# Two-block transformer kernel: in the second block's attention the plain heads go first, and q and k blocks are turned inside it

## The chip, the cores and the metric

One Trainium2 chip, one core. The metric is the device time of one execution in microseconds. Engines by their names: PE is TensorE, ACT ScalarE, DVE VectorE, POOL GpSimd, SP SyncE. All data are fp32; the large projections split each operand into a high and a low fp32r part and make three matmuls of them, attention works in plain fp32.

## What is computed

The reference runs a first block (latent attention and sparse attention, gated, and an MLP) and then a second block of two layers, which is what the change touches:

```
for layer in range(2):
    h = rms_norm(x, g_mix[layer])
    qa, ka, va, qb, kb, vb, qc, kc, vc = split(h @ w_in[layer])    # 4 + 4 + 8 heads of 64
    o_a = differential(qa, ka, va)   # 4 heads: two softmaxes of 32 wide q and k; p0 - lam * p1, then @ v, then a norm per head
    o_b = moba(qb, kb, vb)           # 4 heads; at 512 tokens plain causal attention
    o_c = dilated(qc, kc, vc)        # 8 heads; one softmax with a mask of counts
    x = x + concat(o_a, o_b, o_c) @ w_out[layer]
    x = x + conv_gated_mlp(rms_norm(x, g_ffn[layer]))
```

512 tokens, model width 1024. q, k of each head get a partial rotation first. lam comes from four short vectors per layer by two dot products and two exponentials.

## The kernel before

One program per engine, written out by hand and tied together by counting semaphores. Tokens are four blocks of 128.

**Projection.** The last of six chunks of h @ w_in goes to PSUM banks 4 to 7, the one before it to banks 0 to 3. ACT copies each to z2 (`evacuate`, L1302) and signals `banks_drained`; DVE rotates q and k in z2 (L1727 to L1732) and signals `rotated` per chunk.

**Turning (`two_turns`, L625 to L631).** Attention needs q and k with the head dimension on partitions. Sixteen blocks of 128 columns are transposed by PE, four 128 x 128 transposes each (L889), over the 8 banks in turn, and taken from PSUM by ACT (L1311) or DVE (L1693). `apart` blocks are copied once per head mask: two copies with `halves`, four with `quarters` (the pairs' q); `whole` blocks, the k, once. Even blocks go to ACT, odd ones to DVE. Behind them `meet()` is a barrier of PE, ACT and DVE.

**Attention (`attend`, one version per engine; order by `Plan`, L500).** A job is a head. A score is one tile: 128 queries against the 1 to 4 key blocks of the causal triangle, in the order of query blocks 3, 0, 2, 1, so of 512, 128, 384 and 256 columns. One step issues one score:
- PE: score s (L926), into bank s mod 3; at step s + 3 the transposes of the probabilities (L941), two banks; two steps later their product with v (L952); then whatever `also(step)` holds. Each engine runs its own list in order, and PE does too.
- DVE: mask and row maximum (L1754), into a ring of `M_SLOTS` = 2; `join`; `also`; the copy of the transposed probabilities of query block 3 of single heads (L1774); every fourth value `finish` (L1797, L1803), which scales the head's output into O2.
- ACT: exponential and row sum (L1335), into a ring of `P_SLOTS` = 4 (8 for pairs); `also`; the other copies (L1349).

A head of the differential part is a pair: two scores per query block, lag 5 instead of 3, and `join` on DVE (L1789, L1790, L1792), per query block a reciprocal and a product of one column each, and then b * r + a over the tile. The first five steps behind the lag have filling matmuls, `FILL` = (6, 1, 1, 1, 1) (L899): ident against causal, into bank 7, a result that nobody reads.

`two_jobs` (L575): four pairs (steps 0 to 31), four plain heads (32 to 47), eight dilated heads (48 to 79). `o2_also` turns finished output blocks through bank 3 for the next projection: PE transposes at steps 51, 54, 57, 60, 64, 72, 80 (L1211, which waits until the block before has left the bank), ACT takes the high part one step later (L1576), DVE the low part two steps later (L2142). The norm of the pair heads is at steps 41 (ACT squares, L1581), 44 (DVE), 46 (ACT root, L1584), 48 (DVE). POOL splits weights (L391, L395) two slabs ahead and then waits for PE.

Of the kernel before, what the change touches and what calls it, by code (L numbers as in the profile page):

```python
# [26 lines left out]
D_MODEL, SEQ = 1024, 512  # L27
P = 128
# [65 lines left out]
def build(nc, xT_d, slabs_d, ada_d, c_d, cols_d, rows_d, consts_d, strips_d, pos_d, cpos_d,  # L94
# [5 lines left out]
    with ctx:  # L100
# [24 lines left out]
        rowsum = sb("rowsum", [P, 4, TT])  # L125
# [90 lines left out]
        ring_x = at("ring_x", 32768, [P, 4, SEQ])  # L216
        rope_2 = at("rope_2", 81920, [P, 4, 512])
# [74 lines left out]
        attended, combined = sem("attended"), sem("combined")  # L292
        turned = sem("turned")
# [202 lines left out]
        M_SLOTS, P_SLOTS, PT_SLOTS = 2, 4, 3  # L496
# [3 lines left out]
        class Plan:  # L500


            def __init__(self, jobs):
# [7 lines left out]
                n = len(self.scores)  # L511
                self.slots, self.before, last = [], [], {}
                for i, (m, c, j, v) in enumerate(self.scores):
# [5 lines left out]
                turn = 0  # L519
                for v, (m, j, i) in enumerate(self.values):  # L520
                    pair = len(jobs[m]["q"]) == 2
                    turn = max(turn, i + (PAIR_LAG if pair else TURN_LAG))
# [3 lines left out]
                    if pair:  # L526
                        self.joins.setdefault(i + COMBINE_LAG, []).append(v)
                self.steps = turn + 4

        def masked_slot(ring, u, n):  # L530
            return ring[0][:, u % M_SLOTS, 0:n]

        def probs_slot(ring, slot, n):
            return ring[0][:, M_SLOTS + slot, 0:n] if slot < P_SLOTS else ring[1][:, slot - P_SLOTS, 0:n]
# [41 lines left out]
        for h in range(4):  # L576
            two_jobs.append(job((T2a[:, 2 * h, :], T2a[:, 2 * h + 1, :]), T2b[:, 2 + h // 2, :],
                                lambda kb, h=h: z2[:, 1, kb, 64 * h:64 * h + 64],
                                O2[:, :, 768 + 64 * h:832 + 64 * h], causal))
        for h in range(4):  # L580
            two_jobs.append(job(T2[:, 12 + h, :], T2b[:, h // 2, :],
                                lambda kb, h=h: z2[:, 2, kb, 256 + 64 * h:320 + 64 * h],
                                O2[:, :, 512 + 64 * h:576 + 64 * h], causal))
# [5 lines left out]
        DIFF_SQ, DIFF_SUM, DIFF_ROOT, DIFF_SCALE = 41, 44, 46, 48  # L589
        O2_TURNS = [(51, 6, 4), (54, 7, 4), (57, 4, 6), (60, 5, 8), (64, 0, 10), (72, 1, 12), (80, 2, 14)]  # L590
# [40 lines left out]
        two_turn_chunk = [3] * 4 + [4] * 4 + [1] * 2 + [2] * 2 + [0] * 4  # L631
# [15 lines left out]
        def _(pe):  # L647
# [253 lines left out]
            def attend(jobs, ring, s_banks=S_BANKS, banks_ready=None, also=None):  # L901
# [13 lines left out]
                for step in range(plan.steps):  # L915
# [13 lines left out]
                    if TURN_LAG <= step < TURN_LAG + len(FILL):  # L929
                        release_clock(FILL[step - TURN_LAG])  # L930
# [260 lines left out]
            for layer in range(LAYERS):  # L1191
# [3 lines left out]
                def two_ready(n):  # L1195
                    pe.wait_ge(rotated, 5 * layer + two_turn_chunk[n] + 1)
                    if n in (0, 4):
# [1078 lines left out]
```

## Time and profile before

| | us |
|---|---|
| three runs, median (lowest to highest) | 2388.53 (2387.6 to 2389.87) |
| the profiled execution, its own time | 2389.8 |
| its span | 2388.0 |
| busy in the span: PE, PE weight load | 2285.1 (96%), 1819.2 (76%) |
| busy: DVE, ACT, POOL | 908.6 (38%), 619.4 (26%), 1385.3 (58%) |
| mean granted clock of PE | 0.988 of full |

Read the page from the top: busy time, then 40 slices of the span (the attention of the second block's two layers lies around 1108 to 1240 and 1811 to 1943 us), then the chain. In the timeline each line is a start, a length, the engine, the line of the kernel and what it writes and reads; like instructions are merged, with the first one's shape, and in brackets stands the idle time before, and who ended it. An fp32 matmul is two records.

### The profile page before, as it was taken

The page shows a single profiled execution, that of the slowest core. Times are in us where ns is not written, and L with a number is a line of the kernel's source. Part 1 is how long each engine was busy: PE and PEld are TensorE (multiplying, and loading weights), DVE is VectorE, ACT ScalarE, POOL GpSimd, SP SyncE. Part 2 cuts the span into 40 slices and gives each one's busy share as a digit, 9 for nine tenths or more (in the row PEclk, how much of TensorE's full clock was granted, in tenths as well). Part 3 has the DMA queues.
Part 4 walks back from the last instruction along what each step waited for, and adds up shares of the span by engine and source line. Part 5 has one row for each costly group of instructions (what it writes and reads, how often), then busy time and mean ns, then how long its engine had stood idle before and what let it go on. Part 6 is the DMA issues. An engine that isn't in the chain of part 4 may idle for free.

```text
span 2388.0 us, 29037 instructions
## 1 busy us (share of the span) xinstructions
PE 2285.1 (96%) x10645; PEld 1819.2 (76%) x10645; DVE 908.6 (38%) x1753; ACT 619.4 (26%) x1315; POOL 1385.3 (58%) x462
## 2 busy tenths in 40 slices
PE   4998899999999999999899999999999999999997
PEld 2787687777888888786687888887786787888885
DVE  6835786124111100433743433402425634333302
ACT  2243564012111100113651322301114632223200
POOL 3857501876677777675006777777673026777773
PEclk9999999999999999999999999999999999999998
DMA  8214211322122222122002222222221002222221
GB/s 337 85 71 159 104 57 54 108 100 92 71 99 95 88 102 96 71 96 81 1 2 71 89 105 88 88 106 88 72 104 53 1 19 71 97 97 88 96 98 53
DMA packets 32528, 206.02 MB, mean 86 GB/s; under 512 B 3888, under 2 KB 4144, under 8 KB 11440
## 3 DMA queue, kind: packets, MB, share of 16 engines
q1 hardware_dynamic: 32000, 200.27, 23.4%
q10 hardware_dynamic: 432, 4.46, 0.5%
q8 instruction: 62, 1.02, 0.2%
q14 instruction: 34, 0.28, 0.0%
HBM read 202.61 MB, written 2.10 MB: 86 GB/s over the span
## 4 chain that ended last, share of the span: by engine, by line
PE 83%; issue 7%; DVE 4%; POOL 3%; ACT 1%; DMA 1%; POOLq 0%; DVEq 0%; SPq 0%; ACTq 0%
PE PS L652 25%; PE PS L654 24%; PE PS L653 24%; PE PS L926 3%; PE PS L952 2%; PE PS L941 1%; DMA ada_first<-ada_dram 1%; POOL w_hi L391 1%; POOL w_lo L395 1%; DVE f_lo L1655 1%; PE PS L899 1%; PE PS L982 1%; PE PS L666 1%; DVE t L1624 1%; DVE ada_first L1816 0%
## 5 line engine op out<-in xcount | busy, mean ns | idle before, releaser
L391 POOL TENSOR_TENSOR w_hi<-raw,zero_c 128x2048 fp32r<-128x2048 f32 (+1 forms) x216 | 598.9, 2783 | 941.5 <-PE PS L654 907.3
L395 POOL TENSOR_TENSOR w_lo<-raw,w_hi 128x2048 fp32r<-128x2048 f32 (+1 forms) x216 | 757.4, 3517 | 12.6
L652 PE MATMUL PS<-f_hi,w_hi 128*128 128x512 f32 x1056 | 419.1, 397 | 5.5 <-DVE f_lo L1611 3.6
L654 PE MATMUL PS<-f_hi,w_lo 128*128 128x512 f32 x1056 | 417.8, 396 | 0.0
L653 PE MATMUL PS<-f_lo,w_hi 128*128 128x512 f32 x1056 | 414.7, 393 | 0.0
L652 PEld LDWEIGHTS PS<-f_hi,w_hi 128*128 128x128 f32 x1056 | 198.2, 188 | 52.8 <-issue 6.6
L654 PEld LDWEIGHTS PS<-f_hi,w_lo 128*128 128x128 f32 x1056 | 198.2, 188 | 49.9
L653 PEld LDWEIGHTS PS<-f_lo,w_hi 128*128 128x128 f32 x1056 | 198.2, 188 | 48.1
L2085 DVE SCALAR_TENSOR_TENSOR aux<-PS,cols,aux 128x510 f32<-128x510 f32 (+1 forms) x176 | 123.7, 744 | 237.1 <-ACT aux L1543 230.1
L652 PE MATMUL PS<-a_hi,w_hi 128*128 (+1 forms) x528 | 209.8, 397 | 0.0
L654 PE MATMUL PS<-a_hi,w_lo 128*128 (+1 forms) x528 | 208.9, 396 | 0.0
L653 PE MATMUL PS<-a_lo,w_hi 128*128 (+1 forms) x528 | 207.3, 393 | 0.0
L652 PE MATMUL PS<-w_hi,f_hi 128*128 128x512 f32 x384 | 154.8, 403 | 8.3 <-DVE t L1669 8.3
L653 PE MATMUL PS<-w_lo,f_hi 128*128 128x512 f32 x384 | 153.8, 401 | 0.0
L654 PE MATMUL PS<-w_hi,f_lo 128*128 128x512 f32 x384 | 153.7, 400 | 0.0
L1661 DVE TENSOR_TENSOR xT<-xT,PS 128x512 f32<-128x512 f32 x32 | 21.9, 685 | 284.8 <-PE PS L654 284.1
L654 PEld LDWEIGHTS PS<-a_hi,w_lo 128*128 128x128 f32 x528 | 99.1, 188 | 24.9
L653 PEld LDWEIGHTS PS<-a_lo,w_hi 128*128 128x128 f32 x528 | 99.1, 188 | 24.7 <-issue 0.2
L652 PEld LDWEIGHTS PS<-a_hi,w_hi 128*128 128x128 f32 x528 | 99.1, 188 | 23.0 <-issue 0.2
L952 PEld LDWEIGHTS PS<-z,ring 128*128 128x128 f32 x640 | 80.9, 192 | 18.5 <-ACT ring L1349 12.7
L652 PEld LDWEIGHTS PS<-w_hi,f_hi 128*128 128x128 f32 x384 | 73.4, 191 | 27.4 <-DVE t L1669 9.2
L1549 ACT ACTIVATE a_hi<-PS 128x512 f32 (+1 forms) x66 | 39.6, 599 | 208.4 <-DVE PS L2077 170.3
(387 smaller groups left out, 3610.6 us busy)
## 6 DMA issues: line engine op xcount, KB each, us to landing
raw<-slabs_dram SPq DMA_DIRECT2D x161, 1024.0 KB, 4.8
aux<-ada_dram SPq DMA_DIRECT2D x24, 512.0 KB, 3.8
ada_first<-ada_dram SPq DMA_DIRECT2D x4, 2048.0 KB, 21.7
cmpw<-cmpw_dram ACTq DMA_DIRECT2D x2, 2048.0 KB, 9.5
ada_late<-ada_dram SPq DMA_DIRECT2D x8, 512.0 KB, 3.6
xT<-xT_dram SPq DMA_DIRECT2D x1, 2048.0 KB, 15.9
out_dram<-t SPq DMA_DIRECT2D x4, 512.0 KB, 2.7
crow<-c_dram SPq DMA_DIRECT2D x1, 512.0 KB, 4.5
```

Of the source, the lines that this page charges most:

```text
L391: high = nc.gpsimd.tensor_tensor(w_hi[:, slot, c], raw[:, slot, c], zero[:, 0:c.stop - c.start], ALU.add)
L395: low = nc.gpsimd.tensor_tensor(w_lo[:, slot, c], raw[:, slot, c], w_hi[:, slot, c].bitcast(f32), ALU.subtract)
L652: nc.tensor.matmul(out, a_hi_, b_hi_, start=start, stop=False)
L653: nc.tensor.matmul(out, a_hi_, b_lo_, start=False, stop=False)
L654: return nc.tensor.matmul(out, a_lo_, b_hi_, start=False, stop=stop)
L666: last = nc.tensor.matmul(PS[:, 0, :], mean_w, t[:, k, :], start=not residual and k == 0, stop=k == ks[-1])
L899: nc.tensor.matmul(PS[:, 7, :], ident, causal, start=True, stop=True)
L926: nc.tensor.matmul(PS[:, step % s_banks, 0:128 * nb], jobs[m]["q"][c][:, 128 * j:128 * j + 128], jobs[m]["k"][:, 128 * lo:128 * (lo + nb)] ...
L941: last = nc.tensor.transpose(PS[:, S_BANKS + v % PT_BANKS, 128 * b:128 * b + 128], probs_slot(ring, plan.slots[i], 512)[:, 128 * b:128 * b ...
L952: last = nc.tensor.matmul(PS[:, 6 + m % O_BANKS, 64 * j:64 * j + 64], turned_slot(ring, v, 512)[:, 128 * b:128 * b + 128], jobs[m]["v"](lo ...
L1549: A(a_hi[:, fi, :], g.unsqueeze(1), ACT.Copy).then_inc(act_hi_ready, 1)
L2085: V.scalar_tensor_tensor(out=t[:, sh:], in0=PS[:, bank, 0:SEQ - sh], scalar=cols[:, ds(f + w, 1)], in1=t[:, sh:], op0=ALU.mult, op1=ALU.add)
```

## The change

- `two_jobs` starts with the four plain heads (steps 0 to 15); the pairs take steps 16 to 47, the dilated heads stay at 48 to 79.
- Of the sixteen blocks the four that the plain heads need (two of q in halves, two of k) are turned first, in banks 0 to 3. The other twelve are turned inside `attend` by `also`: PE at steps 0 to 7, 9, 11, 13 and 14, all in bank 3, each once the one before is taken; ACT or DVE takes it at the step after. The first score waits for the first four (`two_operands`), the score of step 16 for all sixteen.
- The barrier goes. DVE waits for ACT's small exponential on a new semaphore, `lam_ready`. The filling matmuls go from this attention (`fill=()`).
- Pairs: `join` works on two tiles at once, one reciprocal and one product over two columns of row sums, then the two wide operations. The lag is longer (joined two steps behind the second tile, transposed five and six behind it), the ring of probabilities has 10 slots, that of masked scores 3, in `ring_y`; `rowsum` has 8 rows.
- `Plan` holds each transpose at least three steps behind that of the fifth value before.
- The pair heads' norm moves to steps 58 to 64, the output turns to 56, 59, 63, 67, 70, 73, 80, in another order.

```diff
-        M_SLOTS, P_SLOTS, PT_SLOTS = 2, 4, 3
+        M_SLOTS, P_SLOTS, PT_SLOTS, P_PAIRS = 2, 4, 3, 10
...
                 for i, (m, c, j, v) in enumerate(self.scores):
-                    slot = i % (2 * P_SLOTS if len(jobs[m]["q"]) == 2 else P_SLOTS)
+                    pair = len(jobs[m]["q"]) == 2
+                    many = any(len(x["q"]) == 2 for x in jobs[max(0, m - 2):m + 1])
+                    slot = i % (P_PAIRS if many else P_SLOTS)
...
+                    slot = i % (M_SLOTS + 1 if pair else M_SLOTS)
+                    self.masks.append(slot)
+                    self.masked_before.append(last_mask.get(slot))
+                    last_mask[slot] = i
...
-                    pair = len(jobs[m]["q"]) == 2
-                    turn = max(turn, i + (PAIR_LAG if pair else TURN_LAG))
+                    if len(jobs[m]["q"]) == 2:
+                        i2 = i + (2 if v % 2 == 0 else 0)
+                        turn = max(turn, i2 + PAIR_LAG + v % 2)
+                        if v % 2:
+                            self.joins[i2 + COMBINE_LAG] = v
+                    else:
+                        turn = max(turn, i + TURN_LAG)
+                    if v >= PT_SLOTS + PT_BANKS:
+                        turn = max(turn, at_step[v - PT_SLOTS - PT_BANKS] + 3)
...
-        DIFF_SQ, DIFF_SUM, DIFF_ROOT, DIFF_SCALE = 41, 44, 46, 48
-        O2_TURNS = [(51, 6, 4), (54, 7, 4), (57, 4, 6), (60, 5, 8), (64, 0, 10), (72, 1, 12), (80, 2, 14)]
+        PAIRS_AT = 16
+        DIFF_SQ, DIFF_SUM, DIFF_ROOT, DIFF_SCALE = 58, 60, 62, 64
+        O2_TURNS = [(56, 4, 2), (59, 5, 4), (63, 0, 10), (67, 6, 8), (70, 7, 8), (73, 1, 12), (80, 2, 14)]
...
-        two_turns = [apart(i, two_src(3, 128 * i), T2, 2 * i, halves) for i in range(4)]
-        two_turns += [whole(i, two_src(4, 128 * i), P, T2[:, 8 + i, :], 1.0) for i in range(4)]
-        two_turns += [apart(i, two_src(1, 256 + 128 * i), T2, 12 + 2 * i, halves) for i in range(2)]
+        two_turns = [apart(i, two_src(1, 256 + 128 * i), T2, 12 + 2 * i, halves) for i in range(2)]
         two_turns += [whole(i, two_src(2, 128 * i), P, T2b[:, i, :], 1.0) for i in range(2)]
+        for i in range(4):
+            two_turns += [apart(i, two_src(3, 128 * i), T2, 2 * i, halves),
+                          whole(i + 1, two_src(4, 128 * i), P, T2[:, 8 + i, :], 1.0)]
         two_turns += [apart(i, two_src(0, 128 * i), T2a, 4 * i, quarters) for i in range(2)]
         two_turns += [whole(i, two_src(0, 256 + 128 * i), P, T2b[:, 2 + i, :], 1.0) for i in range(2)]
+        HEAD = 4
+        turn_step = {step: HEAD + n for n, step in enumerate((0, 1, 2, 3, 4, 5, 6, 7, 9, 11, 13, 14))}
...
-                turn(two_turns, ready=two_ready)
-                meet()
+                def two_turned(n):
+                    pe.wait_ge(turned_act, a0 + counts[n - 1][0])
+                    pe.wait_ge(turned_dve, d0 + counts[n - 1][1])
...
+                def two_operands(step):
+                    if step == 0:
+                        two_turned(HEAD)
+                    if step == TURN_LAG:
+                        pe.wait_ge(banks_drained, at_.drain)
+                    if step == PAIRS_AT:
+                        two_turned(len(two_turns))
...
                 def o2_also(step):
+                    if step in turn_step:
+                        two_turned(turn_step[step])
+                        two_transpose(turn_step[step], 3)
...
+                    if step - 1 in turn_step:
+                        two_taken(turn_step[step - 1])
...
-            def join(ring, plan, m, j, i, nb):
-
-                one, two = (rowsum[:, plan.sums[m][c] % 4, j:j + 1] for c in (0, 1))
-                r = ratio[:, i % 4:i % 4 + 1]
+            def join(ring, plan, jobs, v):
+
+                m = plan.values[v][0]
+                sel = slice(0, 4, 3) if v % 4 == 1 else slice(1, 3)
+                one, two = (rowsum[:, plan.sums[m][c] % 8, sel] for c in (0, 1))
+                r = ratio[:, v % 4 - 1:v % 4 + 1]
                 then(V.reciprocal(r, two))
                 then(V.scalar_tensor_tensor(out=r, in0=r, scalar=lam_c, in1=one, op0=ALU.mult, op1=ALU.mult))
-                a, b = (probs_slot(ring, plan.slots[i - 1 + c], 128 * nb) for c in (0, 1))
-                V.scalar_tensor_tensor(out=b, in0=b, scalar=r, in1=a, op0=ALU.mult, op1=ALU.add).then_inc(combined, 1)
+                for u in (v - 1, v):
+                    _, j, i = plan.values[u]
+                    _, nb = key_range(jobs[m], j)
+                    a, b = (probs_slot(ring, plan.slots[i - 1 + c], 128 * nb) for c in (0, 1))
+                    by = r[:, 1:2] if j > 1 else r[:, 0:1]
+                    V.scalar_tensor_tensor(out=b, in0=b, scalar=by, in1=a, op0=ALU.mult, op1=ALU.add
+                                           ).then_inc(combined, 1)
```

`two_taken(n)` exists on ACT and on DVE: it waits for `turned` and makes the copies of block n, from bank n for the first four and from bank 3 otherwise.

## Rows read from the trace of the kernel before

**Rows 1.** Busy time by stretch (us), the windows view: layer 0's stages, then layer 1.
```profile
1107.78:1120.20 12.42, 7.95 (x66) 7.02 (x65) 9.44 (x14) 11.64 (x20) 8.15 (x2) 0.98 0.32 128
1120.20:1162.62 42.42, 39.92 (x179) 25.44 (x180) 27.34 (x109) 22.84 (x72) 0.00 (x0) 0.97 0.02 8
1162.62:1187.51 24.89, 22.37 (x149) 17.64 (x148) 15.54 (x55) 15.12 (x48) 0.00 (x0) 1.00 0.00 1
1187.51:1239.52 52.01, 50.48 (x364) 42.18 (x364) 32.73 (x102) 33.97 (x104) 0.00 (x0) 1.00 0.01 1
...
1811.09:1942.59 131.50, 120.66 (x753) 92.11 (x751) 85.17 (x278) 83.57 (x243) 8.15 (x2) 0.99 0.04 14
```
In this view the columns are: stretch, length, busy time (and instructions) of PE, PE weight load, DVE, ACT, POOL, then granted clock, DMA share, GB/s.

**Rows 2.** Timeline, the turning ahead of layer 0's attention.
```profile
1108.01 1.91 PE L889 MATMUL PS<-consts,z 128*128 128x128 f32 x16
...
1109.08 2.73 DVE L1693 TENSOR_SCALAR T<-PS,small 128x512 f32<-128x512 f32 x4 [13.18 <-PE PS L889]
...
1112.16 2.41 ACT L1311 ACTIVATE T<-PS,small 128x512 f32<-128x512 f32 x4
```

**Rows 3.** Windows view again, the end of the turning and the first scores.
```profile
1117.50:1120.20 2.70, 0.02 (x1) 0.03 (x1) 2.51 (x4) 2.48 (x5) 0.00 (x0) 0.90 0.78 285
1120.20:1123.00 2.80, 2.80 (x4) 1.25 (x5) 0.92 (x3) 0.00 (x0) 0.00 (x0) 0.50 0.24 99
```

**Rows 4.** Windows view, eight steps of a pair head and four of single heads.
```profile
1143.90:1153.25 9.35, 8.45 (x47) 5.96 (x46) 7.53 (x31) 6.19 (x20) 0.00 (x0) 1.00 0.00 1
...
1219.04:1224.53 5.49, 5.49 (x40) 4.55 (x40) 3.31 (x12) 3.28 (x12) 0.00 (x0) 1.00 0.01 3
```

**Rows 5.** Instruction groups by line and shape, PE in 1120 to 1240: the filling matmuls.
```profile
L899 PE MATMUL PS<-consts 128*128 128x512 f32 x20 | 9.4, 592 | 0.0
```

**Rows 6.** Timeline, one turned output block and the step behind it.
```profile
1204.26 0.61 PE L1211 MATMUL PS<-consts,O 128*128 128x128 f32 x4
...
1204.70 0.81 PE L926 MATMUL PS<-T 128*128 128x384 f32 x2
...
1205.55 0.56 DVE L1754 CUSTOM_DVE_ANT_0 ring<-PS,strip 128x384 f32<-128x384 f32 x1 [0.94 <-PE PS L926]
...
1206.15 0.62 ACT L1335 ACTIVATE ring<-ring,negmax 128x384 f32<-128x384 f32 x1 [1.17 <-DVE negmax L1754]
...
1206.77 0.58 ACT L1576 ACTIVATE o_hi<-PS 128x512 fp32r<-128x512 f32 x1
```

**Rows 7.** Timeline, the scores of 512, 128 and 256 columns in steady state.
```profile
1219.04 1.08 PE L926 MATMUL PS<-T 128*128 128x512 f32 x2
...
1220.46 0.44 PE L926 MATMUL PS<-T 128*128 128x128 f32 x2
...
1222.99 0.65 PE L926 MATMUL PS<-T 128*128 128x256 f32 x2
```

**Rows 8.** Instruction groups by line and shape, masks and exponentials (busy us, mean ns, idle before).
```profile
L1754 DVE CUSTOM_DVE_ANT_0 ring<-PS,strip 128x512 f32<-128x512 f32 x8 | 5.5, 690 | 5.9 <-PE PS L926 5.9
...
L1754 DVE CUSTOM_DVE_ANT_0 ring<-PS,strip 128x256 f32<-128x256 f32 x8 | 3.4, 420 | 0.9 <-PE PS L926 0.9
...
L1754 DVE CUSTOM_DVE_ANT_0 ring<-PS,strip 128x128 f32<-128x128 f32 x8 | 2.3, 290 | 1.7 <-PE PS L926 1.2 <-issue 0.3
...
L1335 ACT ACTIVATE ring<-ring,negmax 128x512 f32<-128x512 f32 x20 | 14.4, 720 | 23.4 <-DVE negmax L1754 23.4
...
L1335 ACT ACTIVATE ring<-ring,negmax 128x128 f32<-128x128 f32 x20 | 7.9, 394 | 2.7 <-DVE negmax L1754 2.6
```

**Rows 9.** Windows view, a place in the first block's attention.
```profile
274.00:276.00 2.00, 1.29 (x12) 1.13 (x11) 1.81 (x6) 0.30 (x3) 2.00 (x2) 1.00 0.25 55
276.00:280.00 4.00, 4.00 (x17) 3.03 (x17) 3.14 (x11) 2.40 (x9) 3.46 (x7) 0.57 0.26 103
```

**Rows 10.** Timeline, a pair's join on DVE up to its wide operation.
```profile
1149.27 0.16 DVE L1789 RECIPROCAL stats<-rowsum 128x1 f32<-128x1 f32 x1
...
1149.80 0.75 DVE L1792 SCALAR_TENSOR_TENSOR ring<-ring,stats 128x512 f32<-128x512 f32 x1
```

More of the change, by code:

```diff
@@ L292, in build @@
         attended, combined = sem("attended"), sem("combined")
+        lam_ready = sem("lam_ready")
         turned = sem("turned")
@@ L576, in build @@
         for h in range(4):
+            two_jobs.append(job(T2[:, 12 + h, :], T2b[:, h // 2, :],
+                                lambda kb, h=h: z2[:, 2, kb, 256 + 64 * h:320 + 64 * h],
+                                O2[:, :, 512 + 64 * h:576 + 64 * h], causal))
+        for h in range(4):
             two_jobs.append(job((T2a[:, 2 * h, :], T2a[:, 2 * h + 1, :]), T2b[:, 2 + h // 2, :],
@@ L1568, in _, with two_taken @@
                 act.wait_ge(lam_summed, layer + 1)
-                A(small[:, 4:6], small[:, 4:6], ACT.Exp)
-                turn(two_turns)
-                meet()
+                A(small[:, 4:6], small[:, 4:6], ACT.Exp).then_inc(lam_ready, 1)
+                turn0 = at_.turn
+                def two_taken(n):
+                    _, _, acts, _ = two_turns[n]
+                    if acts:
+                        act.wait_ge(turned, turn0 + n + 1)
+                    for dst, scale in acts:
+                        A(dst, PS[:, n if n < HEAD else 3, :], ACT.Copy, scale=scale).then_inc(turned_act, 1)
+                for n in range(HEAD):
+                    two_taken(n)
+                at_.turn += len(two_turns)
                 m0 = at_.map
@@ L1751, in attend @@
                         dve.wait_ge(scores_ready, g0 + step + 1)
[L1752 to L1754 removed]
+                        if plan.masked_before[step] is not None:
+                            dve.wait_ge(probs_ready, g0 + plan.masked_before[step] + 1)
+                        V.tensor_tensor_reduce(out=masked_slot(ring, plan.masks[step], 128 * nb),
                                                in0=PS[:, step % s_banks, 0:128 * nb],
@@ L1758, in attend @@
                                                accum_out=negmax[:, step % 8:step % 8 + 1]).then_inc(scores_masked, 1)
-                    for v in plan.joins.get(step, ()):
-                        m, j, i = plan.values[v]
-                        _, nb = key_range(jobs[m], j)
-                        dve.wait_ge(probs_ready, g0 + i + 1)
-                        join(ring, plan, m, j, i, nb)
+                    if step in plan.joins:
+                        v = plan.joins[step]
+                        dve.wait_ge(probs_ready, g0 + plan.values[v][2] + 1)
+                        join(ring, plan, jobs, v)
                     if also:
@@ L2133, in _, with two_taken @@
                         dve.drain().then_inc(lam_summed, 1)
-                turn_counted(two_turns)
-                meet()
+                counts = turned_counts(two_turns)
+                turn0 = at_.turn
+                def two_taken(n):
+                    _, _, _, dves = two_turns[n]
+                    if dves:
+                        dve.wait_ge(turned, turn0 + n + 1)
+                    for dst, scale in dves:
+                        V.tensor_scalar(dst, PS[:, n if n < HEAD else 3, :], scale, None, ALU.mult
+                                        ).then_inc(turned_dve, 1)
+                for n in range(HEAD):
+                    two_taken(n)
+                at_.turn += len(two_turns)
+                at_.turn_a += counts[-1][0]
+                dve.wait_ge(lam_ready, layer + 1)
                 then(V.tensor_tensor(lam_c, small[:, 5:6], small[:, 4:5], ALU.subtract))
```

69 lines of the change are left out of this document (37 added, 32 removed).

## The prediction

> **What bounds the kernel now.** I read the page first: its table has PE busy nearly all the span, so a gain must come from a stretch where PE waits or does work that nobody needs. Next the busy time by stretch, cut at the marks of a layer's attention [rows 1]. The reader should see five stretches of layer 0, end to end: the turning of q and k up to the first score, 12.42 us, with PE busy 7.95; the four heads of pairs, 42.42 (32 score steps); the four plain heads, 24.89 (16 steps); the eight dilated heads, 52.01 (32 steps and the tail). Together 131.74 us; layer 1 takes 131.50, the last row. Everything that the change touches lies in these 2 x 131.7 us, 11% of the span. GpSimd's weight splits are far ahead there and cover nothing.
>
> Then the timeline, for what ends each wait. In the turning, PE makes 16 transposes in 1.91 us, and waits; ScalarE has to copy the last chunk first, load a table, do one small exponential, and takes its first blocks from 1112.16 on at 0.60 us each [rows 2]. In the last 2.70 us ahead of the first score PE does nothing, the granted clock falls, and the first 2.80 us of scores run at 0.50, the lower of the two levels (1.2 GHz) [rows 3]. In the steady stretches, four plain steps take 5.49 us with PE busy all the time, and eight steps of a pair head 9.35 us with PE busy 8.45 and VectorE 7.53 [rows 4]. So plain heads are bound by PE, pairs nearly so.
>
> **Part 1: the shorter opening.** PE transposes 4 blocks instead of 16 ahead of the first score (done at about 1109.9). The first score then waits for ScalarE's three copies: 1112.16 + 3 x 0.60 = 1113.97, with the hand-over 1114.1. VectorE's three, from 1109.1 on, end earlier. Opening: 1114.1 - 1107.8 = 6.3 us for 12.4. The barrier as such cost next to nothing: what ended it were the evictions of all 16. The new wait of VectorE for the exponential (lam_ready, 1112.3) lies ahead of the first mask and is covered by this wait for ScalarE.
>
> **Part 2: the filling matmuls go.** Ten fp32 matmuls of 512 columns, 20 records, 9.4 us [rows 5]. They lay in the first pair head, whose eight steps took 14.8 us (1120.2 to 1135.0) against 9.35 later. This gain is inside the 42.4 and is counted in parts 3 and 4, where I price the steps without them.
>
> **Part 3: twelve blocks turned inside the first sixteen steps.** This is the term that decides. All twelve use PSUM bank 3. At the end of step s PE waits until the block before has been taken from that bank, then transposes the next. That block is taken in step s only after the mask (VectorE) or after mask and exponential (ScalarE) of step s, and these need the score of step s, which PE can issue only behind the transposes of step s-1. So each step with a turn closes a loop over three engines. The trace has this loop once per output block, where it is three or more steps from the next and costs nothing [rows 6]: transposes at 1204.26, score at 1204.70 (+0.44), mask at 1205.55 (+0.85), exponential at 1206.15 (+0.60), copy at 1206.77 to 1207.35 (+0.62, +0.58): 3.09 us. The change puts such turns at steps 0, 1, 2, 3, 4, 5, 6, 7, 9, 11, 13, 14. Each interval is 0.44, the next step's score (1.08, 0.44, 0.86, 0.65 us for 512, 128, 384, 256 columns), its mask (0.69, 0.29, 0.56, 0.42), for ScalarE its exponential (0.72, 0.39, 0.62 for 512, 128, 384), the copies (0.60 on ScalarE or 0.69 on VectorE each; two for a block of halves, four for quarters, one for k) and 0.1 for the return to PE [rows 2, 6 to 8]:
> turn at 0, ScalarE 2 copies, step 1 of 128 columns: 2.86. At 1, VectorE 1, 384: 2.65. At 2, VectorE 2, 256: 2.99. At 3, ScalarE 1, 512: 3.63. At 4, 5, 6 again 2.86, 2.65, 2.99. From 7 to 9: 3.63. From 9, ScalarE 4, 384: 4.97. From 11, VectorE 4, 512: 5.07. From 13, ScalarE 1, 384: 3.17. From 14 to the first score of the pairs, VectorE 1, 256: 2.30. The sum is 39.8, with 0.9 for the first score 40.7 us.
> PE's own work in these steps is 4 x 5.49 + 12 x 0.44 = 27.2 us, so PE waits some 13 us, a little in every step. Where PE waited as much in the first block's attention, busy 1.29 us of 2, the granted clock then read a mean of 0.57 over 4 us, though PE was full again in them [rows 9]. I add 3.5 us: about 1.5 for the first stretch at the low clock behind the opening's 4.2 us of idle PE (before, idle for 2.70 brought a low stretch of 2.80 [rows 3]), and 2 for two or three later falls at 0.5 to 1 us of PE's share of a loop. Bounds: 0 (the clock holds) and 14 (it stays low for all 12 turns and 16 scores: 12 x 0.44 + 4 x 2.16 us more). Part 3: 44.2 us, where the four plain heads had 24.9.
> The Trainium skill (TensorE: Matmul & The Clock Gate, A second HAM failure mode: psum-queue depth-cycling) says that a PE which pauses often for a moment between groups of matmuls because it cycles through PSUM banks can see its clock swing between the levels, and it speaks against this change. The rows just named agree. By the rule taken fully the low clock holds through part 3; that is a rival below.
>
> **Part 4: pairs joined two tiles at a time.** A join spends 0.53 us in two tiny VectorE operations (1149.27 to 1149.80) ahead of the wide one [rows 10]; per head four such become two, so VectorE's 7.53 falls by 1.06 to 6.5, and a join is ready three steps ahead of its transposes instead of behind the next mask. Deeper rings (10 and 3 slots) take the other waits. PE becomes the bound. Its work without waits is the plain head's 5.49 plus a second set of scores, 2 x 1.08 = 2.16: 7.65. I take 8.0 per head and 1 for the change of lag: 33 us for four heads. Ends: 30.6 (7.65 each) and 37.4 (9.35 each, nothing gained).
>
> **Part 5: what is late next.** In the kernel before, the plain heads came behind the pairs and took 24.89 instead of 4 x 5.49 = 21.96: 2.9 us for the shorter lag, with a copy and its transposes late. Now the dilated heads stand there and pay it, and four values are turned in one step (53). The norm of the pair heads with its table loads moves from steps 41 to 48 to 58 to 64, and the output turns crowd from 51-80 to 56-80; both were inside the 52.0, at equal count. Dilated heads: 52.0 + 2.9 = 55 us, ends 53 and 57. The planner's new floor for a turn (three steps behind the fifth value before) binds nothing where all heads are plain, so the first block's attention keeps its order. No DMA and nothing on GpSimd moves; the weight split behind the attention starts later or earlier by as much as the attention ends.
>
> **Sum.** After: 6.3 + 44.2 + 33 + 55 = 138.5; before 131.7. Each layer is longer by 6.8, both by 13.6 us. The profiled execution took 2389.8 us (span 2388.0), so 2403.4; the median of the runs shown is 1.3 lower, and I forecast 2402.
>
> **The rivals.**
> Turns hidden (faster): PE never waits at bank 3, so part 3 costs PE's own 27.2 + 0.9 = 28.1. For it: an output turn with its wait costs nothing beyond PE's work in the trace. Against: those are at least three steps apart, and the loop of 2.7 to 3.6 us is twice PE's 1.37 + 0.44 per step. It decides if the loop is under 1.8 us. 6.3 + 28.1 + 33 + 55 = 122.4, minus 9.3 a layer: 2370. Chance 0.12.
> Balanced: the loop is as priced, but all else sits at its good end: no low clock, 6.3 + 40.7 + 31 + 53 = 131, minus 0.7 a layer: 2387. For it: in the plain stretch before, PE busy nine tenths kept the clock. Chance 0.20.
> Low clock through part 3: all 14 us instead of 3.5, 10.5 a layer more: 2402 + 21 = 2423. For it: the fall named above [rows 9]; against: there it came back within 4 us, while PE was full. By the Trainium skill (same page, What's actually happening) the slow clock is the default and activity lifts it, which is why half-filled steps could leave it low. Chance 0.10.
> The rings and the double join do not shorten the pairs (something else set 9.35, as ScalarE's chain): 4.4 a layer more, 2411. Chance 0.10.
> The forecast's own case, 2394 to 2409: 0.48.
>
> **How the numbers follow.** A difference under 0.2% (4.8 us) is about what a measurement of this kernel can't tell from none. Slower: 0.48 + 0.20 of the two slow rivals, and a little of the balanced case, 0.70. Same: most of the balanced case, 0.14. Faster: the hidden case and the rest of the balanced one, 0.16. The range 2382 to 2420 leaves out the hidden case and the worst of the low clock.
>
> **What would show it.** Right, if the first score comes 6 to 7 us behind the last projection matmul; if turns' transposes in the first eight steps are 2.6 to 3.7 us apart and the two blocks of quarters 5 us; if PE idles some 13 us per layer between score 0 and score 16, released by copies; if a pair head takes about 8 us. Wrong, if those transposes follow at 1.8 us, if score 16 comes within 30 us of score 0, or if the pairs still take 9.3.

## The result, and the profile after it

The changed kernel takes 2422.8 us (median of four runs, 2421.5 to 2426.0) against 2388.1 for the kernel before on the same chip (2386.5 to 2389.9): a ratio of 1.0148, 95% interval 1.0137 to 1.0160, slower by 34.7 us. The forecast was 2402 with a range up to 2420. The direction was right; the size was outside the range, 34.7 us where 13.6 stood in the sum. The execution shown here took 2421.5 us with a span of 2419.7; the one of before had 2388.0.

The windows view of the changed kernel, columns as in [rows 1]: opening, plain heads with the twelve turns, pairs, dilated heads of layer 0, then layer 1 whole.
```profile
1105.52:1111.46 5.94, 1.91 (x18) 1.67 (x16) 3.67 (x4) 5.55 (x9) 5.62 (x2) 0.89 0.29 121
1111.46:1158.36 46.90, 33.09 (x170) 25.16 (x171) 20.57 (x53) 18.64 (x52) 2.49 (x1) 0.76 0.06 23
1158.36:1197.89 39.53, 36.11 (x185) 26.15 (x185) 26.19 (x100) 23.25 (x75) 0.00 (x0) 0.91 0.00 1
1197.89:1254.10 56.21, 51.78 (x364) 42.20 (x364) 35.06 (x110) 35.85 (x107) 0.00 (x0) 1.00 0.01 1
1827.95:1974.40 146.45, 121.84 (x733) 93.66 (x731) 85.56 (x262) 83.17 (x243) 8.11 (x2) 0.92 0.04 13
```
Against 12.42, 42.42, 24.89 and 52.01 [rows 1], the opening is shorter by 6.5 (by 6.2 if both are counted from the first transpose, 1108.01 before), the pairs by 2.9; the plain heads, now first, are longer by 22.0 and the dilated ones by 4.2. Layer 0 takes 148.6 for 131.7, layer 1 146.5 for 131.5: together 31.9 us more, which is the whole difference of the two spans (31.7).

The granted clock of the same kernel, the windows view again: the wait in the opening, the first half of the plain heads, the second, and a place in the pairs; then the last 4 us ahead of the rise at 1134, and the three low stretches in the plain heads of layer 1 (1833.89 to 1881.91).
```profile
1106.00:1110.00 4.00, 1.43 (x14) 1.19 (x11) 2.21 (x4) 3.97 (x7) 3.92 (x2) 1.00 0.31 131
1110.00:1134.00 24.00, 15.59 (x50) 10.80 (x51) 9.54 (x18) 8.55 (x22) 3.95 (x1) 0.50 0.12 44
1134.00:1158.36 24.36, 17.50 (x122) 14.37 (x121) 12.48 (x35) 11.49 (x33) 0.00 (x0) 1.00 0.00 1
1170.00:1179.00 9.00, 8.15 (x32) 6.16 (x30) 4.36 (x19) 5.12 (x18) 0.00 (x0) 0.62 0.00 1
...
1130.00:1134.00 4.00, 4.00 (x19) 3.98 (x20) 0.30 (x2) 2.10 (x6) 0.00 (x0) 0.50 0.00 0
...
1833.89:1837.10 3.21, 3.21 (x8) 1.92 (x8) 3.02 (x3) 0.00 (x0) 2.56 (x1) 0.50 0.00 0
...
1840.60:1857.60 17.00, 12.74 (x42) 8.74 (x42) 4.52 (x12) 4.80 (x13) 0.00 (x0) 0.50 0.01 3
...
1871.30:1874.60 3.30, 3.30 (x12) 2.16 (x11) 1.55 (x4) 0.92 (x5) 0.00 (x0) 0.50 0.02 5
```
In layer 0 the lower level (0.50, 1.2 GHz) is granted for 24 us, behind 4 us in which PE was busy 1.43, and while it lasts PE is busy 15.59 of 24. In layer 1 it comes three times, and adds up to about the same. Before, a low stretch lasted 2.80 us [rows 3].

The turns at steps 0 to 7, from the timeline of PE (start, length; in brackets the idle time before and what ended it):
```profile
1113.32 1.06 PE L1225 MATMUL PS<-consts,z 128*128 128x128 f32 x4
1117.51 1.12 PE L1225 MATMUL PS<-consts,z 128*128 128x128 f32 x4 [2.70 <-ACT T L1621]
1121.21 1.09 PE L1225 MATMUL PS<-consts,z 128*128 128x128 f32 x4 [1.31 <-issue]
1125.05 1.09 PE L1225 MATMUL PS<-consts,z 128*128 128x128 f32 x4 [1.04 <-issue]
1129.96 1.11 PE L1225 MATMUL PS<-consts,z 128*128 128x128 f32 x4 [1.91 <-ACT T L1621]
1133.57 0.84 PE L1225 MATMUL PS<-consts,z 128*128 128x128 f32 x4
1136.37 0.63 PE L1225 MATMUL PS<-consts,z 128*128 128x128 f32 x4 [0.92 <-issue]
1139.32 0.63 PE L1225 MATMUL PS<-consts,z 128*128 128x128 f32 x4 [0.84 <-issue]
```
One round of that loop over three engines, from the turn at 1136.37 to the next, at the full clock (timeline of all engines):
```profile
1136.37 0.63 PE L1225 MATMUL PS<-consts,z 128*128 128x128 f32 x4 [0.92 <-issue]
1136.83 0.60 PE L946 MATMUL PS<-aux,T 128*128 128x256 f32 x2
...
1137.46 0.42 DVE L1810 CUSTOM_DVE_ANT_0 ring<-PS,consts 128x256 f32<-128x256 f32 x1 [1.20 <-PE PS L946]
...
1137.81 1.41 DVE L2204 TENSOR_SCALAR T<-PS,small 128x512 f32<-128x512 f32 x2
```
Turn, score, mask, two copies, next turn: 2.95 us, priced at 2.99. The next two rounds also fit their prices (to 1142.93: 3.61 for 3.63; to 1147.95: 5.02 for 4.97). At the low clock the first four rounds are 4.19, 3.70, 3.84 and 4.91 for 2.86, 2.65, 2.99 and 3.63.

### The profile page after: what moved, and what is told of

It is laid out like the page before. It is cut to its first block, busy times and chain, and to the rows that moved or that the text cites. A ratio compares the mean times of both kernels' runs of the same rounds, so it can differ in the third digit from the quotient of the medians.

```text
span 2419.7 us, 28885 instructions
## 1 busy us (share of the span) xinstructions
PE 2289.0 (95%) x10605; PEld 1824.0 (75%) x10605; DVE 909.0 (38%) x1721; ACT 618.8 (26%) x1315; POOL 1385.7 (57%) x462
## 4 chain that ended last, share of the span: by engine, by line
PE 82%; issue 7%; DVE 4%; POOL 3%; ACT 2%; DMA 1%; POOLq 0%; SPq 0%; DVEq 0%; ACTq 0%
PE PS L672 24%; PE PS L673 24%; PE PS L674 24%; PE PS L946 3%; PE PS L972 3%; PE PS L961 1%; DMA ada_first<-ada_dram 1%; POOL w_lo L397 1%; POOL w_hi L393 1%; DVE f_lo L1711 1%; PE PS L1225 1%; PE PS L1002 1%; PE PS L686 1%; DVE t L1680 1%; DVE ada_first L1878 0%
## 5 line engine op out<-in xcount | busy, mean ns | idle before, releaser
L972 PE MATMUL PS<-z,ring 128*128 128x64 f32 x640 | 89.0, 275 | 5.8 <-ACT ring L1393 5.1
```

Source lines behind the costliest of these rows:

```text
L972: last = nc.tensor.matmul(PS[:, 6 + m % O_BANKS, 64 * j:64 * j + 64], turned_slot(ring, v, 512)[:, 128 * b:128 * b + 128], jobs[m]["v"](lo ...
```

## The experiments

Each is a kernel of its own, timed against the kernel before on the same chip. Where a "+" or "-" line stands for a like one on another engine, one is shown.

**Where the time goes when the turns stay ahead of the attention.** All sixteen blocks turned ahead through eight banks; order, rings, joins and output turns as in the changed kernel.
```diff
-                for n in range(HEAD):
-                    two_transpose(n, n)
+                turn(two_turns, ready=two_ready)
...
-        turn_step = {step: HEAD + n for n, step in enumerate((0, 1, 2, 3, 4, 5, 6, 7, 9, 11, 13, 14))}
+        turn_step = {}
```


> All sixteen blocks turned ahead in eight banks as before, and all else as in the changed kernel (plain heads first, new rings and joins, no barrier, no filler). Theory A (the turns inside cost more than they take from the opening): opening 12 us and score 0 to 16 about 27 us (24.9 of before and 2 for the clock), 39 for what takes 53.1 now: 14 us less a layer, the kernel at about 2395 us, 7 over the kernel before; what is left over it is the dilated part (+4) less the pairs (-3) and the low clock. Rival B (the rings, joins and late o2 turns are what costs): 2410 us or more.

2379.1 us, ratio 0.9963 (0.9950 to 0.9975): faster than the kernel before, and 43.7 us under the changed one. Its stages of layer 0 and its first scores, windows view:
```profile
1106.97:1119.00 12.03, 7.53 (x66) 6.88 (x64) 9.33 (x16) 11.64 (x20) 8.16 (x2) 1.00 0.32 117
1119.00:1139.38 20.38, 20.38 (x123) 15.82 (x123) 11.32 (x41) 11.68 (x40) 0.00 (x0) 0.92 0.05 19
1139.38:1175.98 36.60, 33.03 (x186) 23.58 (x186) 25.91 (x100) 23.47 (x77) 0.00 (x0) 1.00 0.01 1
1175.98:1232.30 56.32, 51.88 (x365) 42.29 (x364) 35.13 (x110) 35.85 (x107) 0.00 (x0) 1.00 0.01 1
...
1119.00:1122.00 3.00, 3.00 (x6) 1.62 (x7) 0.93 (x4) 0.05 (x1) 0.00 (x0) 0.50 0.30 126
```
Moving twelve turns in saved 6.1 us of opening and added 26.5 to plain heads in which PE had nothing idle (20.38 of 20.38) and 2.9 to the pairs. In layer 1 the turns add 27.7 us to the plain heads and nothing to the pairs (36.3 in both kernels). Theory A had the direction; its 2395 was 16 us too high, above all since it took 27 us for plain heads that take 20.4.

**The loop through one bank.** Odd turns of steps 0 to 7 go to bank 7, whose output is not yet written.
```diff
+        def two_bank(n):
+            return n if n < HEAD else 7 if n < 12 and n % 2 else 3
...
-                        two_turned(turn_step[step])
-                        two_transpose(turn_step[step], 3)
+                        n = turn_step[step]
+                        if n == 5:
+                            pe.wait_ge(banks_drained, at_.drain)
+                        else:
+                            two_turned(n - 1 if 5 < n < 12 else n)
+                        two_transpose(n, two_bank(n))
```


> Turns at steps 0 to 7 alternate between banks 3 and 7, so that a turn waits only for the copies of the turn before the last. Theory A (the loop turn, copies, next turn through one bank sets these steps, 3 to 4 us each): turn 0 to turn 7 falls from 26.0 to 17 us or less, score 0 to score 16 from 46.9 to about 37, the kernel to about 2404 us. Rival B (ACT and DVE, with masks, exps and copies, are the bound of a step anyway): the part stays at 43 or more, the kernel at 2416 or more.

2402.5 us, ratio 1.0067 (1.0050 to 1.0084), 20.3 under the changed kernel. Turns of steps 0 to 7 from its timeline:
```profile
1112.59 1.06 PE L1228 MATMUL PS<-consts,z 128*128 128x128 f32 x4
1113.87 1.06 PE L1228 MATMUL PS<-consts,z 128*128 128x128 f32 x4
1116.77 0.68 PE L1228 MATMUL PS<-consts,z 128*128 128x128 f32 x4 [0.57 <-ACT T L1628]
1118.16 0.60 PE L1228 MATMUL PS<-consts,z 128*128 128x128 f32 x4
...
1125.95 0.61 PE L1228 MATMUL PS<-consts,z 128*128 128x128 f32 x4
```
First to eighth turn takes 13.4 us for 26.0; the stage 37.2 for 46.9 (36.7 for 48.0 in layer 1). Theory A holds: the stage is within 0.4 us of its 37, the kernel 1.5 under its 2404. Transposes last 0.6 to 0.7 us again from 1116.77 on, so the clock is back 6 us behind score 0 for 22.5 in the changed kernel (it falls once more, to 0.50 over 1130.60 to 1133.80): part of the gain is the clock's, and this run does not say how much. The stage still takes 17 us more than with all turns ahead; the later turns (steps 9 to 14) stayed on one bank here, and no run broke that part.

**The clock alone.** Filler matmuls into the free half of bank 7, nine ahead of score 0, behind a wait for the last chunk's copy out of that bank, and two ahead of each wait up to step 7.
```diff
+            def keep_clock(n):
+                for _ in range(n):
+                    nc.tensor.matmul(PS[:, 7, 256:512], ident, causal[:, 0:256], start=True, stop=True)
...
+                        if step < 8:
+                            keep_clock(2)
                         two_turned(turn_step[step])
```


> Theory A (the low clock costs 6.3 us a layer in the part with the turns, the loop through bank 3 the rest): with filler matmuls in the opening and before the waits of the turns at steps 0 to 7, the granted clock stays near 1.0 there, score 0 to score 16 goes from 46.9 to about 41 us, and the kernel from 2422.8 to about 2411 us. Rival B (the clock is only what the waiting leaves behind, and the steps are set by ACT and DVE): the clock rises, the part stays within 1 us of 46.9, and the kernel within 3 us of 2422.8. Rival C: the filler stands in the loop, each turn comes 0.4 us later or more, and the kernel is slower than 2423.

2415.9 us, ratio 1.0122 (1.0105 to 1.0139), 6.9 under the changed kernel.
```profile
1108.00:1116.00 8.00, 7.13 (x40) 6.01 (x39) 5.03 (x4) 5.55 (x9) 6.98 (x2) 1.00 0.27 114
1116.00:1148.00 32.00, 26.05 (x158) 19.94 (x157) 13.46 (x37) 14.71 (x40) 1.14 (x1) 1.00 0.09 33
1148.00:1152.00 4.00, 4.00 (x20) 3.37 (x18) 3.04 (x6) 0.98 (x3) 0.00 (x0) 0.57 0.00 0
```
The clock holds up to 1148 (windows view), and the stage takes 42.4 us for 46.9, in layer 1 43.3 for 48.0; the opening gives back 0.8 of it. So the low clock cost at least 4.6 us a layer in this stage: the filler's own time and the stretch at 1148 are still in the 42.4. The kernel gained 6.9 us of theory A's 12. What is missing can be filler as well as too high a price for the clock; this run does not separate them.

**Both at once**, two banks and the nine filler matmuls ahead of score 0.
```diff
+                        keep_clock(9)
                         two_turned(HEAD)
```


> Two banks for the turns at steps 0 to 7, and nine filler matmuls ahead of score 0. Theory A (clock and loop are two prices that add): the clock stays at 1.0 up to 1120 and the part with the turns goes from 37.3 to about 35 us, the kernel from 2402.5 to about 2397. Rival B (with the loop broken the low clock lies beside waits for ACT and DVE): within 2 us of 2402.5.

2403.0 us, ratio 1.0061 (1.0044 to 1.0078): no gain over two banks alone (2402.5), as rival B has it. The opening took 6.8 for 5.9 us, the stage 37.2 for 37.2 (in layer 1 35.8 for 36.7). But the clock was not held: it reads 0.50 over 1121 to 1124 and 0.52 over 1141 to 1144.5. The filler took one of the short low stretches out of each layer's stage, at about its own price. That clock and loop do not add is therefore not shown. With the clock near full in both, one bank (the run before, 0.96 over the stage) and two (0.91) differ by 5.2 us in layer 0, 42.4 and 37.2, and by 7.5 in layer 1: about the loop's own share, with the filler in the one-bank loop counted in.

**The filler of the kernel before.** Only the twenty records of [rows 5] a layer are left out.
```diff
-                attend(two_jobs, (ring_2, ring_x), s_banks=3, also=o2_also)
+                attend(two_jobs, (ring_2, ring_x), s_banks=3, also=o2_also, fill=())
```


> The kernel before without the twenty filler matmuls in the two layers' attention. Theory A (the filler holds the first pair head: 16.6 us to its eighth score and on, where the later ones take 9.35, and without filler the clock is low for some 3 us only, as with all sixteen turned ahead): score 0 to 32 falls from 42.4 to about 39 us, the kernel from 2387 to about 2381. Rival B (without it the clock stays at half speed through the first pair heads, as it does in the changed kernel from 1110 to 1134): 42.4 or more, the kernel at 2390 or more.

2372.8 us, ratio 0.9941 (0.9924 to 0.9958): 15.0 us faster, more than twice what theory A had. Windows of it: the first scores, the pairs, the plain heads.
```profile
1117.40:1120.40 3.00, 2.98 (x4) 1.45 (x5) 1.01 (x4) 0.00 (x0) 0.00 (x0) 0.50 0.23 98
...
1117.40:1154.00 36.60, 32.23 (x158) 21.53 (x159) 26.91 (x109) 22.51 (x72) 0.00 (x0) 0.96 0.02 9
1154.00:1178.90 24.90, 22.39 (x149) 17.63 (x149) 15.55 (x55) 15.08 (x48) 0.00 (x0) 1.00 0.00 1
```
Pairs 36.6 for 42.42 in layer 0, all else equal. The low stretch lasts 3.0 us from the first score on without the filler and 2.9 with it (the 2.80 of [rows 3] are cut just ahead of its end): the filler bought nothing here. In layer 1 the pairs take 35.1 for 42.4, and without the filler the clock reads 1.00 from their first score on.

**The order alone**: kernel before, plain heads first, no filler, output turns and norm set to it.
```diff
...
+        DIFF_SQ, DIFF_SUM, DIFF_ROOT, DIFF_SCALE = 58, 60, 62, 64
+        O2_TURNS = [(56, 4, 2), (59, 5, 4), (63, 0, 10), (67, 6, 8), (70, 7, 8), (73, 1, 12), (80, 2, 14)]
...
```


> The kernel before with only the order changed: plain heads first, no filler, the differential heads finished at steps 58 to 64 and the o2 turns set to it; sixteen turned ahead, the barrier, the old rings and joins. Theory A (new rings and joins are worth some 0.45 us a pair head and little else, and no barrier nothing): about 4 us over the run with all sixteen ahead, 2383. Rival B (they are worth nothing, since the burst at step 53 gives it back): 2379 or less. Rival C (they carry the gain): 2387 or more.

2371.1 us, ratio 0.9931 (0.9915 to 0.9948). That is 8.0 under the run with all sixteen ahead, from which it differs by rings, joins, the wide tile of row sums and the barrier: these cost, where rival B had them at nothing and theory A at a gain.
```profile
1120.30:1140.70 20.40, 20.40 (x123) 15.64 (x123) 11.42 (x42) 11.68 (x40) 0.00 (x0) 0.93 0.03 12
1140.70:1178.50 37.80, 33.67 (x191) 24.34 (x191) 28.37 (x112) 23.69 (x77) 0.00 (x0) 1.00 0.01 2
1178.50:1232.90 54.40, 50.78 (x360) 41.73 (x358) 35.64 (x112) 36.01 (x107) 0.00 (x0) 1.00 0.00 1
```
Pairs 37.8 for 36.6 with the new rings, dilated 54.4 for 56.3: what rings and joins win, the heads behind lose. Within the attention the two are equal to 1 us a layer, so most of the 8 us must lie outside. (Of the 4.8 us between the two profiled spans it does: 2.3 more between the two layers' attentions and 3.2 behind the second, 1.1 less ahead of the first.)

**Rings and joins alone**, on the kernel before, with its order, filler and barrier. The pair heads' norm comes six steps later to make room for the third ring, and the output turns are set to it.
```diff
-        rowsum = sb("rowsum", [P, 4, TT])
+        rowsum = sb("rowsum", [P, 8, TT])
...
+        ring_y = at("ring_y", 116736, [P, 3, SEQ])
...
+                        if v % 2:
+                            self.joins[i2 + COMBINE_LAG] = v
```


> The kernel before with only the deeper rings and the pairs joined two tiles at a time (and the finishing of the differential heads moved 6 steps back, for the room of the third ring). Theory A (rings and joins are worth what the pairs show in the changed kernel, 9.35 to 8.9 us a pair head): the pairs go from 42.4 to about 39.5 us, the kernel from 2388 to about 2382. Rival B (the shorter pairs are owed to their later place, or are given back in the plain heads): 2386 to 2390. Rival C (the burst of turned values that comes with the new plan costs the heads behind the pairs 3 us): 2390 or more.

2396.7 us, ratio 1.0038 (1.0024 to 1.0052): slower by 9.5, rival C. Pairs 41.2 for 42.4, plain heads behind them 28.0 for 24.9 (starts of the scores). Four values are turned in one step here too, 37, with the same two waits of PE (1.33 and 0.55 us) as in the burst of the changed kernel below; behind them the clock reads 0.50 over 1170 to 1173, so part of the 3.1 us is the clock's. And from the last score of layer 0 to the first of layer 1 it took 590.8 us, though little of the change lies there: the kernel before, that without filler and that with the order alone took 588.9, 588.9 and 589.0, the two others with sixteen ahead and the new rings 591.1 and 589.9.

**The burst behind the pairs.** The new plan turns values 31 to 34 in step 53 on two banks; here two at most.
```diff
+                    if at_step[-2:] == [turn, turn]:
+                        turn += 1
```


> All sixteen ahead as in the run before (2379.1 us), and at most two probs tiles turned in a step behind the pairs, where the new plan puts four into step 53. Theory A (the four in one step hold TensorE, 3.8 and 3.1 us at 1182 and 1187 where a step takes 1.2): the dilated heads' scores take 49.5 us for 51.1, the kernel about 2376. Rival B (VectorE, with the last joins, two finished heads and the masks, is what is late there): 2378 to 2381, the stalls move by a step.

2375.4 us, ratio 0.9951 (0.9935 to 0.9968), 3.7 under the run with all sixteen ahead, though the two intervals overlap. The stage itself shows it: from the first dilated score to the end of the last output turn it takes 59.9 us for 61.1, 1.2 less, where theory A had 1.6. The place in the changed kernel's timeline of PE:
```profile
1204.15 0.38 PE L961 MATMUL PS<-consts,ring_x 128*128 128x128 f32 x2
1205.87 0.96 PE L961 MATMUL PS<-consts,ring_y 128*128 128x128 f32 x5 [1.34 <-ACT ring L1393]
1207.37 0.52 PE L961 MATMUL PS<-consts,ring 128*128 128x128 f32 x3 [0.55 <-DVE ring L1829]
```

**64 bytes.** The kernel before with only the wider tile of row sums, which moves the arena behind it by 64 bytes a partition.
```diff
-        rowsum = sb("rowsum", [P, 4, TT])
+        rowsum = sb("rowsum", [P, 8, TT])
```


> The kernel before with the row sums' tile twice as wide, as the change has it, and nothing else: every tile in the arena behind it lies 64 bytes further per partition. Theory A (this is what makes the feed-forward part behind the attention longer in every run with the new rings: its up projection's matmuls run from 62.0 to 308.8 us behind the last score for 61.9 to 307.7, and the down projection to 432.5 for 430.8): the feed-forward part takes 1.7 us more a layer and the kernel 2390 to 2393 us against 2387.5. Rival B (the place of the tiles is nothing, the difference comes with the rest of the new plan): within 1 us of the kernel before.

2393.5 us, ratio 1.0021 (1.0012 to 1.0030): 5.3 us for a tile twice as wide. One line's matmuls behind the attention (count, least, median and greatest ns, first and last start), the kernel before first:
```profile
L652 PE MATMUL PS<-f_hi,w_hi x352: 399/399/470, 1296.2 to 1542.0; 128*128 128x512 f32 x176
L652 PE MATMUL PS<-a_hi,w_hi x176: 399/399/399, 1542.7 to 1665.2; 128*128 x128, 128*128 128x512 f32 x48
```
The same with the wide tile:
```profile
L652 PE MATMUL PS<-f_hi,w_hi x352: 392/397/474, 1297.4 to 1544.1; 128*128 128x512 f32 x176
L652 PE MATMUL PS<-a_hi,w_hi x176: 392/397/400, 1544.8 to 1667.8; 128*128 x128, 128*128 128x512 f32 x48
```
The same 3 x 352 and 3 x 176 matmuls take 245.8 and 122.5 us at one place, 246.7 and 123.0 at the other, 0.4% more with PE full at both. First start to last, the two groups take 370.4 us for 369.0: theory A, with 1.4 us here where it named 1.7, and the kernel 0.5 above its 2390 to 2393. The kernel has such a pair of groups three times (the first block's MLP is the third), so the pace alone gives some 4.2 of the 5.3 us. Against it, layer 0's input projection is 0.5 us shorter with the wide tile (its last 168 first products start over 117.3 us for 117.8). Two of the three up projections of this trace have a low stretch besides (0.50 over 591.80 to 595.10). What makes up the rest of the 5.3 is not traced.

**The tile behind the arena.** The same tile allotted last. The arena does not come to lie as before by it, as the expectation below takes it: nothing stands ahead of it now where the kernel before has 64 bytes of row sums and the changed one 128, so it lies 64 bytes ahead of its place in the kernel before, a third place. On the changed kernel, on the run with spread turns, and on that with the barrier put back.
```diff
+        rowsum = sb("rowsum", [P, 8, TT])
...
+                meet()
```


> The changed kernel with the row sums' tile behind the arena and nothing else. Theory A: 2422.8 less 4 to 5, about 2418. Rival B: 2422 to 2424.

2415.1 us, ratio 1.0115 (1.0100 to 1.0131): 7.7 under the changed kernel, more than the 4 to 5 expected. By the pace above, 4.2 us are the three pairs of groups. In its trace layer 1's plain heads also take 46.6 us for 48.0, with some 19 us at 0.50 for 24. No run tells whether the place of the tiles has to do with that.

> All sixteen ahead, at most two probs tiles turned in a step behind the pairs (2375.4 us), and the wide row sums' tile allotted behind the arena, so that the arena's tiles lie where they lay in the kernel before. Theory A (the 64 bytes cost 1.7 us in each feed-forward part): 2375.4 less 4 to 5, about 2371. Rival B: 2375 to 2376.

2371.4 us, ratio 0.9931 (0.9918 to 0.9945), 4.0 under its like, and equal to the order alone. That run has the barrier and another place of the arena, though, so it is not yet a comparison of rings and joins.

> The kernel of the run with sixteen ahead, spread turns and the row sums' tile behind the arena, with the barrier of TensorE, ScalarE and VectorE put back between the turns and the attention. Theory A (the first score waits for the last copies anyway, the barrier adds only its exchange): 0 to 1 us a layer more than without. Rival B (it also holds the work of lambda and of the strips on VectorE, which now lies behind it): 2 us a layer or more.

2367.6 us, ratio 0.9922 (0.9908 to 0.9935), not slower than without the barrier (the intervals overlap). The opening is 0.2 us longer with it, 12.2 for 12.0: its absence is worth next to nothing. Against the order alone, which has the barrier too, it is 3.5 us lower, with overlapping intervals: whether rings and joins, mended, are worth anything over the old ones stays open. This kernel (sixteen ahead, plain first, no filler, spread turns, tile last) has the lowest median, 20.6 us under the kernel before; the kernel before without its filler has 15.0 of it with one edit.

## Why the prediction was right in direction and wrong in size

**The ledger.** By medians, from before to after: filler out -15.0; order -1.7; new plan, rings, joins, wide tile and no barrier +8.0; twelve turns moved inside +43.7. They add up to +35.0 because each step starts where the last one ends; that this is near the measured +34.7 says only that the kernel before took the same time beside each run, and does not confirm the single steps, which carry 3 us or so of uncertainty each.

**Part 1, the opening: right.** 5.9 us for 6.3. The barrier cost next to nothing, as said (0.2 us).

**Part 2, the filler: not priced.** It was left inside the pairs' 42.4 as a gain to be counted later, so it was never seen that the kernel before pays 5.8 us for it in layer 0's pairs and 7.3 in layer 1's. The rows for it were there: the first pair head took 14.8 us with the filler in it and later ones 9.35, and with the filler the low stretch still lasted 2.80 us [rows 3].

**Part 3, the turns inside: the mechanism right, the size short.** 46.9 and 48.0 us for 44.2, with PE idle 13.8 us in layer 0 where some 13 stood. At the full clock the loop's rounds fit their prices within 0.1 us (one within 0.15); two banks for the first eight turns give 9.7 and 11.4 us, the clock's part included. The term that was mis-sized is the clock: 3.5 us, with 24 us a layer at 0.50 in place of short falls. The first five rounds and the way to the first turn took 6.2 us longer than priced (1.3, 1.0, 0.9, 1.3, 0.8, and 1.0 ahead of the first); holding the clock by filler gave 4.6 net of the filler. If all of that excess is the clock's, the term was 6.2 us in layer 0, not 3.5. I had taken the length of the low stretch from [rows 3] and [rows 9], where PE was full once the low clock had set in; here it stayed idle for a third of the time, 15.59 us busy of 24, and the low clock stayed with it. Ahead of each rise PE had no pause: busy 4.00 of the 4 us up to 1134.00, 3.21 of 3.21 up to 1837.10, 4.00 of 4 up to 1857.60; but 3.4 us without a pause from 1111.46 on brought no rise. The Trainium skill (TensorE: Matmul & The Clock Gate, What's actually happening) has the slow clock as the default that activity lifts; these windows agree. The same page of the Trainium skill (A second HAM failure mode: psum-queue depth-cycling) says that a PE which pauses often while it cycles through PSUM banks sees its clock swing between the levels. Layer 1 did so, with three low stretches of 3.2, 17.0 and 3.3 us in this stage; layer 0 had one of 24. That the level stays low through the whole stage, as the rival took it, happened in neither: from 1134 on the loop goes on with 17.50 us busy of 24.36, and the clock reads 1.00.

**Part 4, the pairs: failed.** 39.5 and 36.3 us for 33. Two steps of it. PE's own work of a pair head was built up as 7.65, the plain head's 5.49 and 2.16 for a second set of scores; measured, the second set is 2.77 (8.26 less 5.49). The row showed 8.45 busy [rows 4], and the joins were not going to take 0.8 of matmuls away:
```profile
1180.08:1188.98 8.90, 8.26 (x48) 5.93 (x48) 6.82 (x29) 6.20 (x20) 0.00 (x0) 1.00 0.00 0
```
A steady pair head of the changed kernel takes 8.90, PE busy 8.26 of it and waiting for ScalarE's copies, once 0.49 us and once 0.14. VectorE fell from 7.53 to 6.82, less than the 1.06 forecast. And the entry into the pairs stalls: behind the first double join and a finished head the masks come late, and PE waits. That stall is there in the run with sixteen ahead too (1.22 us, and the pairs take 36.6) and in layer 1 (0.85, 36.3); in layer 0 of the changed kernel the clock falls a second time behind it (0.62 over 1170 to 1179 above), and the pairs take 39.5:
```profile
1168.15 0.42 DVE L1865 TENSOR_TENSOR O<-PS,stats 128x256 f32<-128x256 f32 x1 [0.44 <-issue]
1168.81 0.42 DVE L1810 CUSTOM_DVE_ANT_0 ring<-PS,consts 128x256 f32<-128x256 f32 x1 [0.23 <-issue]
...
1169.30 1.13 PE L946 MATMUL PS<-aux,T2a 128*128 128x512 f32 x2 [1.22 <-DVE negmax L1810]
```
With filler matmuls ahead the clock read 1.00 over all the pairs, and they took 36.7.

**Part 5, what is late next: right, small.** 56.2 for 55. The burst of four values was named; spreading it gave back 1.2 us of the stage.

**Outside the attention: missed.** The forecast had nothing change there. The tile made twice as wide moves all tiles of the arena behind it by 64 bytes; that alone was 5.3 us on the kernel before. The two profiled executions show 2.3 us more between the layers' attentions and 2.5 less ahead of the first, so in the spans it does not stand out; in the medians, and in the runs with the tile last, it does.

**The sum.** By step and layer, mean of both: part 3 +3.3, pairs +4.9, dilated +1.2, opening -0.4, in all +9.0, the 9.0 us a layer by which the spans exceed the sum (31.7 less 13.6, halved).

**The rivals.** That turns hide (2370) is refuted by the rounds. The low clock throughout (2423) came nearest in number, but it is not what happened: it had 14 us a layer in part 3 and the rest as forecast. That rings and joins do not shorten the pairs (2411) was half true and deserved more than 0.10: in the kernel the dilated heads give back what the pairs win.

## What to carry to other kernels

Work of TensorE that lies beside another engine's copying, as the sixteen transposes here, is free; moved into a stretch where TensorE is full, it costs its own time at least, and through one bank the whole loop over three engines. Two banks gave back 20 of the 44 us here; leaving the transposes where they were gave back all. A filler that keeps the clock is itself work: run once without it, and compare the length of the low stretch with and without. And after widening any tile that is allotted early, time the kernel with that one edit.

## What the runs showed of the hardware that was not expected

The place of tiles changes the pace of TensorE's matmuls: 64 bytes further a partition, 3 x 352 fp32r matmuls of 512 columns took 246.7 us for 245.8, 3 x 176 took 123.0 for 122.5, with no wait in either, and the kernel 5.3 us more. In layer 0 this up projection is 0.9 to 1.0 us slower in all eight traces with the wide tile ahead of the arena. With the tile last, the arena 64 bytes ahead of its first place, the 245.8 us are there again, in the changed kernel as in the two others:
```profile
L672 PE MATMUL PS<-f_hi,w_hi x352: 393/396/473, 1308.2 to 1554.0; 128*128 128x512 f32 x176
```
So of three places 64 bytes apart two give the one pace and the last the other. Why it is slower there is open.

The granted clock stayed at 0.50 for 24 us in which TensorE was busy two thirds of the time, and for 2.9 to 3.0 us where it was full, with or without filler. In the kernel with the lowest median the first 3.5 us of layer 0's scores (1115.30 to 1118.80) read 1.00 and had no low stretch at all, behind 3.30 us with PE busy 0.35, and layer 1 of the kernel before without its filler had none either (1.00 over 1814.70 to 1818.00); no run here tells what made that difference.
